# Value projection and states ahead of the query projection in a head's turn

## The chip, the cores and the metric

The kernel runs on one core of a Trainium2 chip. The metric is the device time of the whole kernel in microseconds (us), the median of several runs. Five engines work side by side, each through a queue of its own in program order: TensorE (PE in the profile; PEld are its weight loads), VectorE (DVE), ScalarE (ACT), GpSimd (POOL) and SyncE (SP, which here only issues DMAs). They meet only at semaphores.

## What is computed

One layer of a streaming encoder over 320 tokens: 256 of a prompt (two tiles of 128) and 64 of a running stream. What the change touches is the gated recurrence of its eight heads (128 keys by 128 values each):

```python
proj = jnp.einsum('btd,dn->btn', h, w_in)
q, f_pre, i_v, g_o, u_a, u_b, gate_a, gate_b = jnp.split(proj, SPLITS, axis=-1)
...
# per head: S_t = diag(f_t) S_{t-1} + k_t v_t^T,  o_t = S_t^T q_t
b = jnp.cumsum(logf, axis=2)
attn = jnp.einsum('bhtd,bhsd,bhtsd->bhts', q, k, decay)
o = (jnp.einsum('bhts,bhsv->bhtv', attn, v)
     + jnp.einsum('bhtd,bhdv->bhtv', q * jnp.exp(b), S))
S_new = (jnp.exp(b_last[:, :, 0, :])[..., None] * S
         + jnp.einsum('bhsd,bhsv->bhdv', k_dec, v))
...
o = rms_norm(o, hg_norm_g)
```

Behind it come a convolution branch, the gates, an output projection, a router and sixteen experts.

## The kernel before

**Stages.** Normalisation of the input, then eight **head turns** (from about 20 to 175 us), then the convolution's projections and the gates, the output projections, the router, and the experts from about 355 us to the end. The head turns 0 and 1 are special (`first`, `first_prev`). TensorE runs turns 2 to 7 in a loop of three passes of two turns (L677); ScalarE and VectorE run turns 2 to 5 in a loop and turns 6 and 7 written out.

**A head turn** is a pipeline over three heads: the current head is projected, the levels and the output of the previous one (`prev`) are computed, and the normalisation of the one before that (`pprev`) is finished. On TensorE one turn from the loop is, in this order:

- `cur_f`: 24 matmuls of 128x320, the forget logits, into PSUM bank 0;
- `rms` (L646): a matmul against ones, the sum of squares for `pprev`, into bank 1. It waits for `prev_square` on ScalarE (L1235);
- `levels` (L591): 55 small matmuls of the previous head. It waits for `xr_ready` (VectorE's `query_side`, L1658) and `xk_ready` (GpSimd's `key_side`, L1504);
- `prev_kT` (L614): three transposes;
- `cur_q` (L569): 24 matmuls of 128x320, the query projection, into bank 1. It waits for `rstd_ready`, ScalarE's Ln of bank 1 (L1247), since the sums of `rms` lie in that bank;
- `prev_states` (L622): three matmuls into bank 7;
- `cur_v` (L583): the value projection, into bank 3, 48 passes in the trace;
- `prev_out` (L630): the output of the previous head.

The forget and query projections split inputs and weights into a high and a low part. ScalarE makes the high part of a weight (`w_high`, L1111), VectorE the low one (`w_low`, L1605), and `wlo_ready` counts the low parts.

**ScalarE's turn** is, in this order: `forget` (L1158 to L1164, on the forget logits), `pprev_rms` (L1247, L1248), `key_exp`, `prev_states` (copies of the transposes), `w_high` of the next head's forget weights, `prev_cross`, `q_copy` (L1172: bank 1 to SBUF, signals `q_sb`), `prev_sa` (L1228: first part of bank 7 to SBUF), `level_exp` (L1192: one exponential over 2176 columns, signals `E_ready`), `tile_exp`, `w_high` of the next head's query weights, `v_copy`, `prev_square` (L1235), `store_states` (two DMA issues).

**VectorE's turn**: `forget_in` and the scan, the masks of the previous head, `level_decay` (L1645: seven differences, the input of `level_exp`), `pprev_out`, `w_low` of the next head's forget weights, `prev_final` (L1701, L1703: the new states), `query_side` (L1658: the exponentials times the query, seven instructions), `carry_side`, `w_low` of the next head's query weights. **GpSimd's turn**: `key_decay` (L1490), `level_sums`, `key_side` (L1504, seven instructions).

**SyncE** loads the three weight columns of a head when `v_done` says that the head before the last is projected (L420), and the incoming state when `so_ready` and `o_done` allow it.

The order of the work is written by hand; no scheduler moves anything.

Of the kernel before, what the change touches and what calls it, by code (L numbers as in the profile page):

```python
# [115 lines left out]
def signal(eng, ins, sem, value):  # L116

    ins.then_inc(sem, 1)
    eng.wait_ge(sem, value)


def build(nc, a, o):
    with ExitStack() as ctx:
# [3 lines left out]
        def sem(name):  # L127
            return ctx.enter_context(nc.semaphore(name))
# [44 lines left out]
        def carve(first, *sizes):  # L173
# [65 lines left out]
        cur = [v.rearrange("p (w t e) -> p w t e", w=2, t=3) for v in (cur0, cur1)]  # L239
# [12 lines left out]
        xh_ready, xl_ready, whi_ready, wlo_ready, uhi_ready, ulo_ready, thi_ready, tlo_ready = (  # L252
            sem(n) for n in ("xh_ready", "xl_ready", "whi_ready", "wlo_ready", "uhi_ready", "ulo_ready", "thi_ready", "tlo_ready"))
# [274 lines left out]
        def _(pe):  # L528
            def mm(out, lhsT, rhs, start, stop):
                return pe.matmul(out, lhsT, rhs, start=start, stop=stop)  # L530
# [11 lines left out]
            def project(bank, hi, lo):  # L542

                for k in range(KT):
                    for j, (w, x) in enumerate(((hi, xhk), (lo, xhk), (hi, xlk))):
                        last = mm(ps[:, bank, 0:T], w[:, k * P:k * P + P], x[:, k, :], k == 0 and j == 0, k == KT - 1 and j == 2)
                return last

            def first_f():
                for k in range(KT):  # L550
                    pe.wait_ge(xh_ready, XH[k])
                    if k == 0:
                        pe.wait_ge(xh_ready, XT_A[0])
                    mm(ps[:, 0, 0:T], wh[:, k * P:k * P + P], xhk[:, k, :], k == 0, False)
                for k in range(KT):
                    pe.wait_ge(xl_ready, XL[k])
                    mm(ps[:, 0, 0:T], wh[:, k * P:k * P + P], xlk[:, k, :], False, False)
                pe.wait_ge(wlo_ready, 1)
                for k in range(KT):
                    last = mm(ps[:, 0, 0:T], wl[:, k * P:k * P + P], xhk[:, k, :], False, k == KT - 1)  # L560
                last.then_inc(h["f_done"], 1)

            def cur_f(i, b, first):
                pe.wait_ge(wlo_ready, 2 * (2 * i + b) + 1)
                if not first:
                    pe.wait_ge(h["ls_ready"], 2 * i + b)
                project(0, piece(wh, 0), piece(wl, 0)).then_inc(h["f_done"], 1)

            def cur_q(i, b, first, after_rms):  # L569
                pe.wait_ge(wlo_ready, 2 * (2 * i + b) + 2)  # L570
                if not first:
                    pe.wait_ge(h["q_sb"], 2 * i + b)
                if after_rms:
                    pe.wait_ge(h["rstd_ready"], 2 * i + b - 1)
                project(1, piece(wh, 1), piece(wl, 1)).then_inc(h["q_done"], 1)

            def value_tile(b, t):
                t0, n = TILES[t]
                for k in range(KT):
                    last = mm(ps[0:n, 3, t * P:t * P + P], xT[:, k, t0:t0 + n], sh[:, b, 3, k, :], k == 0, k == KT - 1)  # L580
                return last

            def cur_v(i, b, first):  # L583
                pe.wait_ge(wh_in[b], i * 48 + (16, 48)[b])
                if not first:
                    pe.wait_ge(h["v_sb"], 2 * i + b)
                value_tile(b, 0)
                value_tile(b, 1)
                value_tile(b, 2).then_inc(h["v_done"], 1)
# [24 lines left out]
            def prev_kT(i, b, first):  # L614
                pe.wait_ge(h["kdec_ready"], 2 * i + b + 1)
                if not first:
                    pe.wait_ge(h["so_ready"], 2 * i + b)
                for t, (t0, n) in enumerate(TILES):
                    last = pe.transpose(ps[0:n, 7, t * P:t * P + P], hkde[:, t0:t0 + n], ident)
                last.then_inc(h["kT_done"], 1)  # L620

            def prev_states(i, b):  # L622
                n1 = 2 * i + b
                pe.wait_ge(h["kT_sb"], n1 + 1)
                pe.wait_ge(h["v_sb"], n1 + 1)
                for t, (t0, n) in enumerate(TILES):
                    last = mm(ps[:, 7, t * P:t * P + P], hkT[0:n, t, :], hV[0:n, t, :], True, True)
                last.then_inc(h["s_done"], 1)
# [24 lines left out]
            def head_turn(cur, prev, pprev, first=False, first_prev=False):  # L653

                if first:
                    first_f()
                else:
                    cur_f(*cur, first)
                if first or first_prev:
                    cur_q(*cur, first, False)  # L660
                if first_prev:
                    prev_kT(*prev, True)
                    levels(*prev, True)
                    prev_states(*prev)
                if pprev:
                    rms(*pprev)
                    levels(*prev, False)
                    prev_kT(*prev, False)
                    cur_q(*cur, False, True)
                    prev_states(*prev)  # L670
                cur_v(*cur, first)
                if prev:
                    prev_out(*prev, first_prev)

# [402 lines left out]
        def _(act):  # L1077
# [88 lines left out]
            def q_copy(i, b, first):  # L1166
                n = 2 * i + b
                act.wait_ge(h["q_done"], n + 1)
                if not first:
                    act.wait_ge(h["a_done"], 2 * n - 2)  # L1170
                    act.wait_ge(h["qeb_ready"], n - 1)
                signal(act, act.activation(hq[:, b, :], ps[:, 1, 0:T], ACT.Copy, scale=QSCALE), h["q_sb"], n + 1)  # L1172
# [32 lines left out]
            def prev_states(i, b, first):  # L1205
                n = 2 * i + b
                act.wait_ge(h["kT_done"], n + 1)
                if not first:
                    act.wait_ge(h["s_done"], n)
                pc.turn(n)  # L1210
                pc(act.activation(hkT[:, 0:2, :], ps[:, 7, 0:256].rearrange("p (t n) -> p t n", t=2), ACT.Copy))
                signal(act, act.activation(hkT[0:64, 2, :], ps[0:64, 7, 256:384], ACT.Copy), h["kT_sb"], n + 1)

            def prev_cross(i, b, first):
                n = 2 * i + b
                act.wait_ge(h["am_ready"], 2 * n + 1)
                if not first:
                    act.wait_ge(h["o_done"], n)
                signal(act, act.activation(hAS[0:BLK, 0:2, BLK:P], ps[0:BLK, 4:6, LW:LW + BLK], ACT.Copy), h["ac_ready"], n + 1)

            def prev_sa(i, b, first):

                n = 2 * i + b
                act.wait_ge(h["s_done"], n + 1)
                if not first:
                    act.wait_ge(h["so_ready"], n)
                    act.wait_ge(h["o_done"], n)
                signal(act, act.activation(hSA, ps[:, 7, 0:P], ACT.Copy), h["sa_sb"], n + 1)  # L1228
# [21 lines left out]
            def head_turn(cur, nxt, prev, pprev, first=False, first_prev=False):  # L1250
                forget(*cur, first or first_prev)
                if pprev:
                    pprev_rms(*pprev)
                key_exp(*cur)
                if prev:
                    prev_states(*prev, first_prev)
                if nxt:
                    w_high(*nxt, 0)
                else:
                    u_high(0, 0)  # L1260
                if prev:
                    prev_cross(*prev, first_prev)
                q_copy(*cur, first or first_prev)
                if prev:
                    prev_sa(*prev, first_prev)
                if first:
                    w_high(*nxt, 1)
                level_exp(*cur)
                tile_exp(*cur, first)
                if nxt is None:  # L1270
                    u_high(0, 1)
                    u_high(1, 0)
                    u_high(1, 1)
                elif not first:
                    w_high(*nxt, 1)
                v_copy(*cur, first)
                if prev:
                    prev_square(*prev, first_prev)
                    store_states(*prev)
# [935 lines left out]
```

## Time and profile before

| | us |
|---|---|
| median of 3 runs | 866.62 (865.63 to 866.66) |
| the profiled execution, its own time | 866.5 |
| its span, from the first to the last instruction | 864.6 |
| PE busy | 819.3 (95%) |
| DVE, ACT, POOL busy | 420.4, 239.5, 79.9 |

The span is 2 us shorter than the execution's time. Of the chain that ended last, PE has 60% of the span, DVE 19%, ACT 9% and DMA 9%. In the head turns PE is busy 98% of the time; how the other engines stand in a turn is seen only in their timelines. In a timeline a row shows when the engine started, for how long, and in brackets the idle time ahead of it and what ended that. All matmuls have the line L530, a helper; they are told apart by their tiles: `split_w` are the forget and query projections, `ring,xT` the value projection, `ring` the levels, `cst,ar` at L619 the transposes, `ar,ones` the sum of squares, `ar` x6 the states.

### The profile page before, as it was taken

What the parts mean: (1) busy time and instruction counts of PE and PEld (TensorE: products, weight loads), DVE (VectorE), ACT (ScalarE), POOL (GpSimd) and SP (SyncE); (2) the same over time, 40 slices, a digit from 0 to 9 for tenths busy, and PEclk for the clock granted to TensorE, in tenths of its full rate; (3) what the DMA queues carried; (4) which work ended last, traced back from release to release, by engine and by line L of the source; (5) the groups of instructions that cost most, each with busy time, mean ns of one, the idle gap of its engine ahead of it and who ended that gap; (6) DMA issues with size and microseconds to landing.
All of it is one profiled execution on the core that took longest, in us unless ns stands there. A gap on an engine that the chain in (4) does not pass through costs nothing.

```text
span 864.6 us, 13003 instructions
## 1 busy us (share of the span) xinstructions
PE 819.3 (95%) x5072; PEld 527.6 (61%) x5072; DVE 420.4 (49%) x703; ACT 239.5 (28%) x377; POOL 79.9 (9%) x141
## 2 busy tenths in 40 slices
PE   4999999999999999999999999999999999998892
PEld 2989889989999867576453353534435344352351
DVE  6788889988999973886010201202112021120127
ACT  6666665665455425110101010000100000000011
POOL 1344455430000000000000000000000000000000
PEclk8999999999999999999999999999999999999996
DMA  9322222244333834549979999999999999999991
GB/s 333 144 83 85 82 82 82 106 160 161 135 140 127 338 147 169 225 159 420 423 328 381 430 424 431 428 426 428 427 430 428 428 428 430 427 427 428 428 397 66
DMA packets 33015, 251.09 MB, mean 290 GB/s; under 512 B 4750, under 2 KB 8206, under 8 KB 20938
## 3 DMA queue, kind: packets, MB, share of 16 engines
q1 hardware_dynamic: 30432, 249.17, 70.8%
q10 hardware_dynamic: 2538, 1.32, 0.5%
q8 instruction: 29, 0.48, 0.2%
q14 instruction: 16, 0.13, 0.0%
HBM read 247.99 MB, written 2.48 MB: 290 GB/s over the span
## 4 chain that ended last, share of the span: by engine, by line
PE 60%; DVE 19%; ACT 9%; DMA 9%; issue 2%; ACTq 1%; DVEq 0%; SPq 0%
PE ps L530 58%; DMA ring<-in_w_up_e 8%; DVE ar L1767 4%; DVE ring L1645 4%; DVE split_t L1774 3%; ACT ring L1192 2%; ACT ar L1202 1%; DMA ring<-in_w_in 1%; DVE ar L1681 1%; ACT split_w L1111 1%; DVE ar L1692 1%; PE ps L917 1%; DVE ar L1636 1%; ACTq L1241 1%; ACT ar L1164 1%
## 5 line engine op out<-in xcount | busy, mean ns | idle before, releaser
L530 PE MATMUL ps<-ring,ar 128*64 128x512 f32 (+1 forms) x1056 | 219.4, 569 | 3.3 <-DMA ring<-in_w_gate_e 1.6
L530 PE MATMUL ps<-ring,xT 128*64 128x512 f32 (+2 forms) x896 | 159.9, 459 | 5.3 <-DMA ring<-in_w_gate_e 3.6
L530 PEld LDWEIGHTS ps<-ring,ar 128*64 128x64 f32 x1056 | 73.6, 137 | 133.8 <-issue 123.0
L530 PEld LDWEIGHTS ps<-ring,xT 128*64 128x64 f32 (+1 forms) x896 | 78.6, 152 | 79.0 <-issue 69.2
L530 PE MATMUL ps<-split_x,split_t 128*128 128x320 f32 x672 | 101.1, 311 | 0.5 <-DVE split_t L1774 0.5
L530 PEld LDWEIGHTS ps<-split_x,split_t 128*128 128x128 f32 x672 | 98.6, 188 | 2.5 <-issue 1.4
L2067 DVE TENSOR_TENSOR ar<-ar,ps 128x512 f32<-128x512 f32 (+1 forms) x42 | 28.8, 685 | 137.9 <-PE ps L530 136.1
L530 PE MATMUL ps<-split_x,split_w 128*128 128x320 f32 x480 | 80.0, 323 | 5.9 <-ACT ar L1247 1.8
L530 PEld LDWEIGHTS ps<-split_x,split_w 128*128 128x128 f32 x480 | 73.4, 194 | 10.6 <-ACT split_x L1146 2.1
L1767 DVE SCALAR_TENSOR_TENSOR ar<-ar,params 128x350 f32<-128x350 f32 x116 | 67.7, 584 | 4.1
L2034 DVE SCALAR_TENSOR_TENSOR out_lo<-ps,ar,out_hi 128x1024 fp32r<-128x1024 f32 x7 | 9.0, 1284 | 104.7 <-ACT out_hi L1409 104.7
L530 PE MATMUL ps<-ar 128*64 128x1 f32 (+6 forms) x354 | 48.8, 292 | 0.0
L530 PEld LDWEIGHTS ps<-ar,mid 128*128 128x128 f32 x384 | 43.7, 192 | 7.8 <-issue 7.8
L530 PE MATMUL ps<-ar,mid 128*128 128x128 f32 x384 | 45.4, 277 | 0.0
L530 PEld LDWEIGHTS ps<-ar 128*64 128x64 f32 (+2 forms) x354 | 34.1, 155 | 11.8 <-issue 9.3
L530 PE MATMUL ps<-mid,ring 128*128 128x320 f32 x128 | 34.9, 432 | 0.0
L1490 POOL TENSOR_TENSOR ring<-ar 128x160 f32<-128x160 f32 (+1 forms) x56 | 28.3, 505 | 64.1 <-DVE ar L1636 60.3
L1409 ACT ACTIVATE out_hi<-ps,ar 128x1024 fp32r<-128x1024 f32 x7 | 7.8, 1114 | 94.2 <-PE ps L530 94.2
L2048 DVE TENSOR_TENSOR ar<-ar,ps 128x1024 f32<-128x1024 f32 x7 | 8.6, 1222 | 52.1 <-PE ps L530 52.1
L1392 ACT ACTIVATE ar<-ps 128x1024 f32<-128x1024 f32 x8 | 8.2, 1026 | 91.2 <-PE ps L530 91.2
L1504 POOL TENSOR_TENSOR ring<-ring,ar 128x160 f32<-128x160 f32 (+1 forms) x56 | 30.4, 543 | 25.5 <-ACT ring L1192 16.3
L1658 DVE TENSOR_TENSOR ring<-ring,ar 128x160 f32<-128x160 f32 (+1 forms) x56 | 30.5, 544 | 2.1 <-ACT ring L1192 0.2
(225 smaller groups left out, 839.5 us busy)
## 6 DMA issues: line engine op xcount, KB each, us to landing
ring<-in_w_gate_e SPq DMA_DIRECT2D x31, 2048.0 KB, 20.8
ring<-in_w_up_e SPq DMA_DIRECT2D x31, 2048.0 KB, 16.0
ring<-in_w_down_e SPq DMA_DIRECT2D x26, 2048.0 KB, 19.9
ring<-in_w_in SPq DMA_DIRECT2D x56, 512.0 KB, 4.3
ring<-in_w_down_end SPq DMA_DIRECT2D x3, 2048.0 KB, 35.5
ring<-in_w_o_a SPq DMA_DIRECT2D x8, 512.0 KB, 5.5
ring<-in_w_out SPq DMA_DIRECT2D x1, 4096.0 KB, 14.4
ar<-in_w_down_e SPq DMA_DIRECT2D x6, 512.0 KB, 16.1
```

The costliest lines, as they stand in the source:

```text
L530: return pe.matmul(out, lhsT, rhs, start=start, stop=stop)
L917: last = pe.transpose(ps[:, k // 4, (k % 4) * P:(k % 4) * P + P], eh[:, k * P:k * P + P], ident)
L1111: signal(act, act.activation(piece(wh, q), sh[:, b, q].rearrange("p k n -> p (k n)"), ACT.Copy), whi_ready, 2 * n + q + 1)
L1192: signal(act, act.activation(X[b], X[b], ACT.Exp), h["E_ready"], n + 1)
L1490: ins = pool.tensor_tensor(xv, bv[:, :, hs - 1:hs].to_broadcast([P, w // (2 * hs), hs]), bv[:, :, 0:hs], ALU.subtract)
L1504: ins = pool.tensor_tensor(xv, xv, kv, ALU.mult)
L1645: ins = dve.tensor_tensor(xv[:, :, hs:2 * hs], bv[:, :, hs:2 * hs], bv[:, :, hs - 1:hs].to_broadcast([P, w // (2 * hs), hs]), ALU.subtract)
L1658: ins = dve.tensor_tensor(xv, xv, qv, ALU.mult)
L1767: vc(dve.scalar_tensor_tensor(acc, uc[:, c, j:j + CW], vt[:, c, j:j + 1], acc, ALU.mult, ALU.add))
L1774: signal(dve, dve.tensor_tensor(t_lo[1 - b][q][1], stl[:, b, 8 * q:8 * q + 8].rearrange("p k n -> p (k n)"), t_hi[1 - b][q][0], ALU.subtract),
L2034: signal(dve, dve.scalar_tensor_tensor(out_lo[:, :], ps[:, 6:8, :].rearrange("p b n -> p (b n)"), gs, hiF, ALU.mult, ALU.subtract), e["eos ...
L2067: signal(dve, dve.tensor_tensor(yv, yv, ps[0:c, 4 + j % 2, :], ALU.add), e["y_added"], 6 * n + j + 1 + 6 * late)
```

## The change

On TensorE, in the turns of the loop, the value projection and the states now stand ahead of the query projection. The value projection gets one more wait, for the low part of the current head's query weights: `v_done` frees the buffer from which that part is computed. On ScalarE, in the same turns, the copy of the state `prev_sa` stands ahead of `q_copy`. Turns 0 and 1 keep their order.

```diff
             def cur_v(i, b, first):
                 pe.wait_ge(wh_in[b], i * 48 + (16, 48)[b])
+                pe.wait_ge(wlo_ready, 2 * (2 * i + b) + 2)
                 if not first:
                     pe.wait_ge(h["v_sb"], 2 * i + b)
...
                     rms(*pprev)
                     levels(*prev, False)
                     prev_kT(*prev, False)
+                cur_v(*cur, first)
+                if pprev:
+                    prev_states(*prev)
                     cur_q(*cur, False, True)
-                    prev_states(*prev)
-                cur_v(*cur, first)
                 if prev:
                     prev_out(*prev, first_prev)
...
                 if prev:
                     prev_cross(*prev, first_prev)
+                if prev and not first_prev:
+                    prev_sa(*prev, first_prev)
                 q_copy(*cur, first or first_prev)
-                if prev:
+                if first_prev:
                     prev_sa(*prev, first_prev)
```

TensorE, the second turn of the loop's body from the transposes to the output, before (`split_w` is the query projection, `ring,xT` the value projection, `ar 128x128 x3` ahead of it the states, the last two rows the output):

```order
L619 MATMUL ps<-cst,ar 128x128 x2
L619 MATMUL ps<-cst,ar 64x128
L570 REGISTER_ALU
L530 MATMUL ps<-split_x,split_w 128x320 x24
L530 MATMUL ps<-ar 128x128 x3
L584 REGISTER_ALU
L530 MATMUL ps<-ring,xT 128x128 x16
L530 MATMUL ps<-ring,xT 64x128 x8
L635 ISA
L530 MATMUL ps<-ar 128x128 x3
L530 MATMUL ps<-ar 128x64 x2
```

The same place after:

```order
L620 MATMUL ps<-cst,ar 128x128 x2
L620 MATMUL ps<-cst,ar 64x128
L584 REGISTER_ALU
L585 REGISTER_ALU
L530 MATMUL ps<-ring,xT 128x128 x16
L530 MATMUL ps<-ring,xT 64x128 x8
L530 MATMUL ps<-ar 128x128 x3
L530 MATMUL ps<-split_x,split_w 128x320 x24
L636 ISA
L530 MATMUL ps<-ar 128x128 x3
L530 MATMUL ps<-ar 128x64 x2
```

The query projection moved from right behind the transposes to right ahead of the output.

ScalarE in the same turn, from the cross block's copy (`prev_cross`) to `level_exp`, before (L1172 is `q_copy`, L1228 `prev_sa`, L1192 `level_exp`):

```order
L1219 ACTIVATE ar<-ps 64x2x64
L1170 ISA
L1171 REGISTER_ALU
L1172 ACTIVATE ar<-ps 128x320
L1228 ACTIVATE ar<-ps 128x128
L1192 ACTIVATE ring<-ring 128x2176
L1200 ACTIVATE ar<-ar 128x320
```

The same place after (the lines lie two further down in the file):

```order
L1221 ACTIVATE ar<-ps 64x2x64
L1230 ACTIVATE ar<-ps 128x128
L1172 ISA
L1173 REGISTER_ALU
L1174 ACTIVATE ar<-ps 128x320
L1194 ACTIVATE ring<-ring 128x2176
L1202 ACTIVATE ar<-ar 128x320
```

`q_copy` and `prev_sa` changed places; `q_copy` is now the instruction right ahead of `level_exp`, and it stood ahead of it before too. VectorE, GpSimd and SyncE have the same instructions in the same order as before.

## Rows read from the trace of the kernel before

**Rows 1.** Windows, core 0: stretch, length, busy us of PE, PEld, DVE, ACT, POOL, granted clock, DMA share, GB/s

```profile
75.31:95.26 19.95, 19.57 (x193) 17.81 (x192) 17.20 (x30) 12.56 (x24) 9.46 (x18) 1.00 0.29 90
...
174.50:198.00 23.50, 21.71 (x197) 20.41 (x197) 20.27 (x33) 13.22 (x22) 7.05 (x9) 1.00 0.48 166
```

**Rows 2.** Waits between 56 and 180 us: who waited for whom, total us, times, longest

```profile
ACT ring L1192 <- DVE ring L1645: 24.5, 6, 4.3
...
PE ps L530 <- ACT ar L1247: 1.8, 4, 0.6
```

**Rows 3.** Timeline of TensorE in turn 3: start, length, what, idle before

```profile
79.08 0.78 PE L530 MATMUL ps<-ar,ones 128*128 128x320 f32 x2
79.87 0.92 PE L530 MATMUL ps<-ring 128*64 128x64 f32 x24
...
82.69 0.55 PE L619 MATMUL ps<-cst,ar 128*128 128x128 f32 x3
83.60 3.76 PE L530 MATMUL ps<-split_x,split_w 128*128 128x320 f32 x24 [0.36 <-ACT ar L1247]
87.20 1.02 PE L530 MATMUL ps<-ar 128*128 128x128 f32 x6
88.15 5.73 PE L530 MATMUL ps<-ring,xT 128*128 128x128 f32 x48
93.89 1.44 PE L530 MATMUL ps<-ar 128*128 128x128 f32 x10
...
99.03 0.81 PE L530 MATMUL ps<-ar,ones 128*128 128x320 f32 x2
```

**Rows 4.** Timeline of ScalarE from turn 3 into turn 4

```profile
80.11 0.44 ACT L1158 ACTIVATE ar<-ps 128x320 f32<-128x320 f32 x1 [1.17 <-issue]
...
87.58 0.44 ACT L1172 ACTIVATE ar<-ps 128x320 f32<-128x320 f32 x1 [0.23 <-PE ps L530]
88.30 0.28 ACT L1228 ACTIVATE ar<-ps 128x128 f32<-128x128 f32 x1 [0.28 <-PE ps L530]
92.91 2.02 ACT L1192 ACTIVATE ring<-ring 128x2176 f32<-128x2176 f32 x1 [4.33 <-DVE ring L1645]
...
98.53 0.44 ACT L1235 ACTIVATE ar<-ps 128x320 f32<-128x320 f32 x1
...
100.48 0.44 ACT L1158 ACTIVATE ar<-ps 128x320 f32<-128x320 f32 x1 [1.51 <-issue]
```

**Rows 5.** Timeline of VectorE in turn 3

```profile
88.67 4.16 DVE L1645 TENSOR_TENSOR ring<-ar 128x128 f32<-128x128 f32 x7
...
95.94 3.92 DVE L1658 TENSOR_TENSOR ring<-ring,ar 128x128 f32<-128x128 f32 x7
...
101.39 1.23 DVE L1605 TENSOR_TENSOR split_w<-ring,split_w 128x1024 fp32r<-128x1024 f32 x1
```

**Rows 6.** Timeline of VectorE in turn 1

```profile
55.01 3.92 DVE L1658 TENSOR_TENSOR ring<-ring,ar 128x128 f32<-128x128 f32 x7 [0.17 <-ACT ring L1192]
```

**Rows 7.** Timeline of GpSimd in turn 1

```profile
55.06 4.37 POOL L1504 TENSOR_TENSOR ring<-ring,ar 128x128 f32<-128x128 f32 x7 [3.14 <-issue]
```

**Rows 8.** Timeline of TensorE in turn 2, the first of the loop

```profile
62.58 0.55 PE L619 MATMUL ps<-cst,ar 128*128 128x128 f32 x3
```

**Rows 9.** Timeline of ScalarE, `level_exp` of turn 2 and turn 7, `prev_square` of turn 7

```profile
72.87 2.02 ACT L1192 ACTIVATE ring<-ring 128x2176 f32<-128x2176 f32 x1 [4.21 <-DVE ring L1645]
...
171.70 2.03 ACT L1192 ACTIVATE ring<-ring 128x2176 f32<-128x2176 f32 x1 [3.80 <-DVE ring L1645]
...
179.53 0.44 ACT L1235 ACTIVATE ar<-ps 128x320 f32<-128x320 f32 x1
```

**Rows 10.** Timeline of TensorE behind the last head turn

```profile
180.11 0.78 PE L530 MATMUL ps<-ar,ones 128*128 128x320 f32 x2 [1.79 <-ACT ar L1235]
...
183.64 0.55 PE L619 MATMUL ps<-cst,ar 128*128 128x128 f32 x3
183.94 3.77 PE L530 MATMUL ps<-split_x,split_w 128*128 128x320 f32 x24
```

## The prediction

> **What bounds the kernel now.** First the windows of the head turns: TensorE is busy 19.57 of 19.95 us in turn 3, so it looks like the bound [rows 1]. The waits name what the change aims at: the query projection waits for the Ln of the sums, 1.8 us in four turns [rows 2]. But the same view has a far longer line: ScalarE's `level_exp` waits for VectorE's `level_decay`, 24.5 us in six turns. That idle time is no reserve. `level_exp` stands in a ring of waits of its own: from it ScalarE works straight through to `prev_square`, issues the stores, starts `forget` of the next turn, and VectorE goes on from there to the next `level_decay`. In numbers [rows 4]: `level_exp` 92.91 to the end of `prev_square` 98.97 is 6.06 us, on to `forget` at 100.48 is 1.51 (1.17 ahead of the `forget` at 80.11, where no loop end lies between), and from a `forget` (80.11) to its `level_exp` (92.91) 12.80. Sum 20.0 to 20.4 us, which is what a turn takes: from `level_exp` of turn 2 at 72.87 to that of turn 7 at 171.70 is 98.83, or 19.77 a turn [rows 9]. TensorE's `rms` also hangs on this ring: in turn 4 it starts at 99.03, 0.06 after `prev_square` [rows 3, 4]. So two rings, TensorE's own work and the one over ScalarE and VectorE, are both about a turn long, and what counts is whether the change lengthens a ring through both.
>
> **The edits, one by one.** No matmul is added or removed. The register instructions on TensorE change places; I price them at nothing, as they lie within the gaps between groups counted below.
>
> The *removed wait*: the transposes start at 82.69, the query projection at 83.60 [rows 3]; where nothing held the next group it started 0.30 after the transposes (183.64 to 183.94) [rows 10]. I take 0.35 for a group with other waits. The value projection can then start at 83.04 instead of 83.60, a gain of 0.56 on TensorE's side in such a turn.
>
> The *added wait* in the value projection, for the low query weights, costs nothing: VectorE makes them at the end of its turn, behind `query_side` and `carry_side`, done 6.7 us after `query_side` starts (95.94 to 101.39 + 1.23 [rows 5]), so about 9 us after `level_exp` starts; the value projection stands 10 us after it (sum below). If it did bite, the levels ahead of it would mostly have waited already. Behind it in the queue stand the states, the query and the output. The other waits of the moved groups have been met by then too: the copies of values and transposes are early in ScalarE's turn, and the next turn's loads are issued behind `v_done`, which now comes earlier.
>
> The *moved query projection* is where the cost lies. Its end, and with it `q_copy`, comes later by the value projection (88.15 to 93.89, 5.74) and the states (87.20 to 88.15, 0.95) less the 0.56 won: 6.1 us [rows 3]. `q_copy` started at 87.58 and `level_exp` behind it in the same queue could not start before 92.91 anyway [rows 4], so 5.33 less 0.47 for `q_copy` itself, 4.86, is cover. The rest, 1.2 us, is on the path. Directly for turn 2: transposes 62.58 [rows 8], +0.35 +5.74 +0.95, from a query projection's start to `q_copy` 3.98 (83.60 to 87.58), +0.44 +0.03 gives 74.07 for `level_exp` against 72.87: **1.20 us late**. `level_exp` needs nothing of the query; it is late only because `q_copy` stands ahead of it.
>
> The *swap of prev_sa and q_copy* takes 0.28 us [rows 4] off the way behind `q_copy`, and moves it to where ScalarE waits for the query anyway. Without the swap the price would be that much higher each turn; it is in the sum.
>
> **The new ring.** From then on every turn closes a ring over both engines. From `level_exp` to the end of `prev_square` 6.06 [rows 4]; to `rms` 0.06; `rms` to levels 0.79; levels to transposes 2.82; to the value projection 0.35; value projection 5.74; states 0.95; query projection to `q_copy` 3.98; `q_copy` to `level_exp` 0.47 [rows 3, 4]. Sum **21.22 us**, against 19.77 on average before: 1.45 more in each of the five steps from turn 2 to turn 7, 7.25. With the 1.20 of turn 2: **8.45 us** at the `level_exp` of turn 7.
>
> What is second in line now? `level_decay` would be ready 20.0 to 20.4 after the last `level_exp`, 0.8 to 1.2 us early, so the old ring no longer binds. VectorE's `query_side` began 3.03 us after `level_exp` (95.94 less 92.91) only since VectorE was late with other work [rows 4, 5]; now it can begin as soon as the exponential ends, and GpSimd's `key_side` with it. That happened in turn 1 already: 55.01 for 3.92 and 55.06 for 4.37 [rows 6, 7]. So the keys are done 2.02 + 0.13 + 4.37 = 6.5 us after `level_exp`, 6.7 with a handover of 0.2, and the levels want them at 6.06 + 0.06 + 0.79 = 6.91. A margin of 0.2: it holds, barely.
>
> **What follows the turns.** `rms` of the tail waits for `prev_square` of turn 7 and has waited 1.79 us for it already [rows 9, 10]; that wait gives no cover, since the value waited for is late by the full amount. All that comes after, the convolution, gates and experts with their loads, is released by this work, so I carry the shift to the end whole: 866.5 + 8.45 = 874.95, say **874.9**. The execution of 866.5 is 0.1 under the median of the runs, which changes nothing. A measurement of this kernel can tell about 0.2%, 1.7 us, from no change.
>
> **Bounds of this case.** Low: in the turns that ScalarE has written out the handovers are shorter, and the gap behind the transposes may be 0.30 and not 0.35; 0.25 off in each of five turns and 0.3 off turn 2 gives 6.9, a time of 873.4. High: the gap behind the transposes as long as 0.6 with register work ahead of the value projection, a handover of 0.14 (179.97 to 180.11 [rows 9, 10]) in place of 0.06, and one of 0.1 between `q_copy` and `level_exp`: 0.4 in each of six turns, 2.4 more, or 877.3.
>
> **The rivals.**
>
> *Faster: TensorE's own work is the bound (chance 0.03).* For it: 98% busy [rows 1], and the result of the query projection is not used by VectorE until 95.94 [rows 5]. Then 0.56 us in each of six turns is won, 3.4 us: 863.1. It decides at one point: `q_copy` must be done by 92.9, so the query projection must end by 92.2 in turn 3. On TensorE's sequence it ends at 83.04 + 5.74 + 0.95 + 3.76 = 93.5. I see nothing that brings it 1.3 us earlier. The Trainium skill, page "Perfetto Trace Analysis", section "Optimization Strategy", says to take the most contended engine, find the gaps on it, and make what it waits for start sooner or end sooner. By that rule this change is right and the time falls as in this rival; the trace does not agree that the gap is the limit, since the ring over `level_exp` is as long as TensorE's turn.
>
> *No change (0.04).* The 1.2 us of a turn would be cover that I have missed, or would be given back behind the turns: 866.5 to 868.2. Against it: ScalarE's work between `level_exp` and `prev_square` has no gap, and `rms` starts 0.06 behind it.
>
> *Less, 868.2 to 873.4 (0.08).* The ring closes but is shorter, or part of the shift is absorbed by the loads and the DMA-heavy experts. Each tenth in the ring is worth 0.5 us.
>
> *More, over 877.3 (0.05).* The levels wait for `key_side` or `query_side`, which now run fully side by side. In turn 1 they did so at 3.92 and 4.37 us, as against 3.92 in turn 3 with a later start [rows 5 to 7], so they hardly hold each other up. If they ran one after the other, the levels would start at 2.15 + 3.92 + 4.37 = 10.4 in place of 6.91: 3.5 us in each of five turns, a time of 892. The Trainium skill, page "GPSIMD Engine Reference", section "Key points", states that GpSimd shares its SBUF interfaces with VectorE and contends with instructions of two SBUF inputs, which both of these are. By the rule at its hardest this is the outcome; turn 1 speaks against it.
>
> **How the numbers follow.** The forecast's case, 873.4 to 877.3, has 0.80. I put the range at 872.8 to 877.4, which leaves out both rivals below and most of the two at its edges. Slower by over 0.2% has 0.80 + 0.08 + 0.05 = 0.93, within 0.04, faster 0.03.
>
> **What would show it.** In the profile after: (1) the idle time ahead of `level_exp` is gone, and ahead of `q_copy` ScalarE idles about 3 us for TensorE; (2) TensorE idles 1.4 to 1.6 us ahead of `rms` in turns 3 to 7, released by `prev_square`, and not at all behind the transposes; (3) `level_exp` to `level_exp` 21.2 us; (4) `query_side` starts about 2.1 us after `level_exp`; (5) the granted clock of the turns stays at 1.00, as it did with 1.79 us of idle in the stretch behind them [rows 1]; (6) all behind turn 7 is shifted as a block by about 8 us. I am wrong if `level_exp` still waits for VectorE, if the levels wait for GpSimd or VectorE, or if the shift at turn 7 is not found again at the end.

## The result, and the profile after

The changed kernel takes 877.92 us (median of 4 runs, 875.59 to 879.81) against 866.64 (4 runs): a ratio of 1.0128, 95% interval 1.0116 to 1.0141. It is 11.3 us slower, where 8.45 were forecast, and the median lies 0.5 us above the range. The profiled execution took 878.53 us, 12.0 more than the profiled one of before; its span is 876.7. In the file of after ScalarE's lines lie 2 and VectorE's and GpSimd's 4 further down: `q_copy` is L1174, `prev_sa` L1230, `level_exp` L1194, `prev_square` L1237, `query_side` L1662, `key_side` L1508.

The waits between 56 and 190 us (total us, times, longest), which answer to [rows 2]:

```profile
POOL ring L1508 <- ACT ring L1194: 24.4, 6, 4.6
ACT ar L1174 <- PE ps L530: 21.2, 6, 3.6
ACT ar L1230 <- PE ps L530: 15.7, 6, 3.2
...
PE ps L530 <- ACT ar L1237: 10.8, 7, 4.0
```

The line of 24.5 us, `level_exp` waiting for `level_decay`, is gone. In its place ScalarE waits for the query projection, 3.5 us a turn, and TensorE waits for `prev_square` in every turn. ScalarE's timeline from turn 3 to turn 4 answers to [rows 4]:

```profile
95.37 0.44 ACT L1174 ACTIVATE ar<-ps 128x320 f32<-128x320 f32 x1 [3.57 <-PE ps L530]
95.84 2.02 ACT L1194 ACTIVATE ring<-ring 128x2176 f32<-128x2176 f32 x1
...
101.47 0.44 ACT L1237 ACTIVATE ar<-ps 128x320 f32<-128x320 f32 x1
...
117.02 2.02 ACT L1194 ACTIVATE ring<-ring 128x2176 f32<-128x2176 f32 x1
```

`level_exp` follows `q_copy` by 0.47 us with no wait of its own, and comes back after 21.18 us. TensorE's timeline of the same turn, which answers to [rows 3]:

```profile
84.37 0.55 PE L620 MATMUL ps<-cst,ar 128*128 128x128 f32 x3
84.75 5.63 PE L530 MATMUL ps<-ring,xT 128*128 128x128 f32 x48
90.31 1.13 PE L530 MATMUL ps<-ar 128*128 128x128 f32 x6
91.37 3.78 PE L530 MATMUL ps<-split_x,split_w 128*128 128x320 f32 x24
95.53 1.44 PE L530 MATMUL ps<-ar 128*128 128x128 f32 x10 [0.38 <-DVE mid L1714]
96.90 3.79 PE L530 MATMUL ps<-split_x,split_w 128*128 128x320 f32 x24
101.96 0.81 PE L530 MATMUL ps<-ar,ones 128*128 128x320 f32 x2 [1.28 <-ACT ar L1237]
```

The value projection starts 0.38 after the transposes with nothing in between, so the wait that the change removes is really gone. The idle time has only moved, to the front of `rms`, and has grown. One more wait is new, 0.38 ahead of the output (`pprev_out` on VectorE, L1714), but it ends well inside the time that TensorE then spends waiting for `rms`.

Up to here the chain is as forecast; only the idle time stands in two places. Ahead of `rms` it is 0.76 to 1.74 us in turns 3 to 7, where 1.4 to 1.6 were forecast. Together with the new wait ahead of the output it is 1.65 to 1.77 a turn. What else was not forecast is seen behind the last turn. TensorE, rows that answer to [rows 10]:

```profile
188.71 1.40 PE L530 MATMUL ps<-ar,ones 128*128 128x320 f32 x2 [4.02 <-ACT ar L1237]
190.05 1.55 PE L530 MATMUL ps<-ring 128*64 128x64 f32 x24
...
194.93 0.55 PE L620 MATMUL ps<-cst,ar 128*128 128x128 f32 x3
195.23 3.76 PE L530 MATMUL ps<-split_x,split_w 128*128 128x320 f32 x24
```

The group of 24 level matmuls takes 1.55 us where it took 0.92 a turn earlier and before [rows 3]. From `rms` to the next projection it is 6.52 us (188.71 to 195.23), against 3.83 before (180.11 to 183.94 [rows 10]). The windows (columns as in [rows 1]; the granted clock is the number third from the end) say why:

```profile
75.89:96.90 21.01, 19.47 (x193) 17.83 (x192) 17.34 (x30) 12.44 (x24) 9.69 (x17) 1.00 0.25 86
...
188.70:195.20 6.50, 6.49 (x79) 5.57 (x79) 1.66 (x3) 1.00 (x2) 0.00 (x0) 0.55 0.08 21
```

Granted clock 0.55: TensorE ran at its lower level of 1.2 GHz for most of that stretch, after 4.02 us without work. So the 12.0 us of the profiled execution are: 0.5 us from before the first changed turn (the forget projection of turn 2 starts at 55.29 in place of 54.75), 8.1 us in the turns (`level_exp` of turn 7 at 180.33 against 171.70, less that 0.5), 2.7 us of lower clock, and 0.7 us further behind. The 0.5 are scatter: in experiments 7 and 8, whose code is the same as before up to turn 7, this projection starts at 55.31 and 55.64. The 0.7 lie in the router's part, where the clock fell in both profiled executions, before and after. Its stretch from the small matmuls of 16 columns to the next long group takes 10.57 us before (388.49 to 399.06), 11.27 after (399.74 to 411.01), and 9.31 in the execution of experiment 3, where the clock stayed up there. TensorE after, in that stretch:

```profile
401.58 2.30 PE L530 MATMUL ps<-ar,xT 128*128 128x16 f32 x16
403.72 2.06 PE L530 MATMUL ps<-mid,cst 128*128 128x512 f32 x2
```

The clock falls within the first of these rows (1.00 from 402.0 to 402.8, 0.50 from 403.5 to 409.5), and no idle time is recorded ahead of them. Before, the same first row took 1.85 us, and the clock fell only after the second one and an idle time of 0.76 us (0.56 from 394 to 396).

### The profile page after: what moved, and what is told of

It reads as the page before. It is cut to its first block, busy times and chain, and to the rows that moved or that the text cites. A ratio compares the mean times of both kernels' runs of the same rounds, so it can differ in the third digit from the quotient of the medians.

```text
span 876.7 us, 13004 instructions
## 1 busy us (share of the span) xinstructions
PE 824.6 (94%) x5072; PEld 532.2 (61%) x5072; DVE 421.7 (48%) x703; ACT 239.4 (27%) x377; POOL 80.6 (9%) x141
## 4 chain that ended last, share of the span: by engine, by line
PE 69%; DVE 14%; DMA 8%; ACT 7%; issue 1%; ACTq 0%; SPq 0%; DVEq 0%
PE ps L530 67%; DMA ring<-in_w_up_e 8%; DVE ar L1771 5%; DVE split_t L1778 3%; ACT ring L1194 2%; ACT ar L1204 1%; ACT split_w L1113 1%; DVE ring L1649 1%; PE ps L919 1%; DMA ar<-in_x_prompt 1%; DVE ring L1558 1%; DVE mid L1788 0%; DVE ring L1563 0%; PE ps L620 0%; PE ps L909 0%
## 5 line engine op out<-in xcount | busy, mean ns | idle before, releaser
L1508 POOL TENSOR_TENSOR ring<-ring,ar 128x160 f32<-128x160 f32 (+1 forms) x56 | 30.9, 551 | 33.5 <-ACT ring L1194 24.4
L1662 DVE TENSOR_TENSOR ring<-ring,ar 128x160 f32<-128x160 f32 (+1 forms) x56 | 30.5, 544 | 5.7 <-ACT ring L1194 4.0
```

The lines of the kernel that those rows point to most:

```text
L1508: ins = pool.tensor_tensor(xv, xv, kv, ALU.mult)
L1662: ins = dve.tensor_tensor(xv, xv, qv, ALU.mult)
```

## The experiments

Every run was timed beside the kernel before on the same chip; the kernel before had medians of 866.45, 866.3 and 867.03 us in the three groups.

**1. The changed kernel once more.**

> The changed kernel once more, as the standard for the others of this call: 877 to 878.5 us. Theory: about 8.4 us come from the turns (level_exp to level_exp 21.1 us) and about 2.7 us from TensorE at its lower clock (granted 0.55 between 191 and 195 us) behind the 4.0 us idle ahead of the first rms after the turns. If that is so, a run in which the clock does not fall there should show 875 us.

876.89 us (875.12 to 878.38). The two executions with a mean clock of 0.991 took 875.49 and 875.12 us, the two with 0.980 and 0.981 took 878.30 and 878.38. That points to the clock, but the mean is a weak sign: the kernel before has means of 0.984 to 0.993 in the three groups, and its times do not follow them. The step between `level_exp` of turn 2 (74.78) and turn 6 (159.38) is 21.15 us a turn. But from turn 6 to turn 7 it is 22.60 (159.38 to 181.98), and the windows show that the clock fell in a second place, in turn 7, behind an idle time of only 1.72 us ahead of `rms`:

```profile
165.50:171.00 5.50, 5.43 (x79) 4.95 (x80) 4.30 (x8) 4.12 (x8) 0.36 (x1) 0.69 0.51 187
190.30:195.70 5.40, 5.34 (x78) 4.56 (x79) 1.44 (x2) 1.00 (x2) 0.00 (x0) 0.68 0.09 26
```

My expectation knew of one place only. The step of turn 7 grew by 1.5 us, and behind the last turn `rms` to the next projection took 5.37 us.

**2. Filling TensorE's idle time behind the last turn.**

```diff
             conv_value(0)
+            pe.wait_ge(h["q_sb"], 8)
+            project(1, u_hi[0][0][1], u_lo[0][0][1])
             rms(3, 0)
```

> The changed kernel, with one more projection (24 matmuls of 128x320, 3.8 us) on TensorE in the 4.0 us in which it idles behind the last turn; its result in bank 1 is overwritten by rms and never read, so the outputs are the same. Theory (the clock fell because of that idle time): the granted clock stays at 1.00, rms and levels take 3.8 us in place of 6.5, and the time is 2.7 us below the changed kernel, 875.0 to 875.4. Rival (the 2.7 us are lost whatever TensorE does, or the added matmuls themselves delay rms): 877.5 to 879.

876.10 us (874.00 to 877.43), 0.8 below the changed kernel of the same group, so the number I gave was missed. The profiled execution explains it: where the idle time was filled the clock stays up, and `rms` to the next projection is back at 3.84 us; in turn 7, where nothing was filled, it fell again. Windows of turn 7 and of the tail:

```profile
165.20:170.70 5.50, 5.46 (x79) 4.99 (x80) 4.30 (x8) 4.12 (x8) 0.33 (x1) 0.69 0.52 194
190.00:194.00 4.00, 3.95 (x80) 3.47 (x81) 1.60 (x2) 1.00 (x2) 0.00 (x0) 1.00 0.12 35
```

In this execution the mechanism holds for its own place, and the theory had to take in the second.

**3. Filling both places.**

```diff
                 if pprev:
+                    pe.wait_ge(h["q_sb"], 2 * cur[0] + cur[1])
+                    mm(ps[:, 1, 0:T], ones, xT[:, 0, :], True, True)
                     rms(*pprev)
                     levels(*prev, False)
```

and the tail's filling as above.

> The changed kernel with TensorE's idle time filled in both places where its clock was seen to fall: the extra projection behind the last turn as in the run with the filled tail, and in turns 2 to 7 one extra matmul of 128x320 against ones (0.78 us) ahead of rms, whose result rms overwrites. The added work is never read, so the outputs are the same. Theory (all that the changed kernel costs above the ring's 8.4 us is the clock in these two places): granted clock 1.00 from 30 to 350 us, every execution near 874.5 (873.8 to 875.2), none of the 877 to 879 that the changed kernel and the filled tail also show. Rival (the spread comes from elsewhere, the experts' loads or the start): the same 874 to 877.4 as with the filled tail alone.

874.12 us, and the five executions lie within 873.76 and 874.79. Granted clock over all of the turns and the stage behind them:

```profile
30.00:350.00 320.00, 311.91 (x2447) 283.59 (x2446) 267.48 (x433) 174.51 (x271) 77.82 (x136) 1.00 0.36 128
```

TensorE does more work here than in the changed kernel, and the kernel is faster and no longer spreads: 874.12 against 876.89, which is 2.8 us across two groups, or 2.5 us by the two ratios to the kernel before. The result of the added matmuls is never read, so they can pay only by way of the clock. Not all of the gain need be theirs: the router's stretch, where nothing was filled, takes 9.31 us in this execution and 10.69 in that of experiment 1. What is left over the kernel before is a ratio of 1.0084 (1.0070 to 1.0098), some 7 us beside the 8.45 computed; `level_exp` of turn 7 stands at 179.88 against 171.70, with the same 21.14 us a turn.

**4. `level_exp` ahead of `q_copy`.**

```diff
                 if prev and not first_prev:
                     prev_sa(*prev, first_prev)
+                    level_exp(*cur)
                 q_copy(*cur, first or first_prev)
...
-                level_exp(*cur)
+                if first or first_prev:
+                    level_exp(*cur)
```

> The changed kernel with level_exp ahead of q_copy on ScalarE in turns 2 to 7, TensorE's order as changed. Theory (the loss in the turns comes only from level_exp standing behind q_copy, which waits for the query projection): the ring through TensorE opens, what remains is ScalarE's ring with q_copy's 0.47 us now inside it, 20.2 us a turn, and 869 to 869.8 us with the clock at 1.00. Rival (the order on TensorE costs by itself, levels or query_side start late since the query ends later): 21 us a turn and 874 or more.

870.33 us (868.56 to 872.80), 6.6 below the changed kernel, with the same order on TensorE. ScalarE in turn 3:

```profile
93.64 2.02 ACT L1194 ACTIVATE ring<-ring 128x2176 f32<-128x2176 f32 x1 [2.74 <-DVE ring L1651]
95.82 0.44 ACT L1174 ACTIVATE ar<-ps 128x320 f32<-128x320 f32 x1 [0.17 <-ACT ring L1194]
```

`level_exp` waits for VectorE again, as in [rows 4], and comes every 20.32 us (73.10 to 174.69 in five steps; 20.2 expected). The median is 0.5 above what I gave, and for a reason met already: behind the last turn TensorE idles 2.62 us, the clock falls, and `rms` to the next projection takes 6.72 us in the profiled execution; the one with a mean clock of 0.993 took 868.56. So the loss in the turns does not come from TensorE's order as such. It comes from the place of one copy in ScalarE's queue: the turn is 0.8 us shorter than in the changed kernel, and the 0.55 us that it is still above 19.77 are about the 0.47 of that copy, which now stands behind `level_exp` in ScalarE's own ring.

**5 and 6. Each half of the change alone.** First TensorE's part, with ScalarE's old order (`q_copy`, then `prev_sa`):

> TensorE's new order with ScalarE's old one (q_copy, prev_sa, level_exp). Theory: prev_sa's 0.31 us (0.28 and a handover) come into the ring in six turns: 1.9 us above the changed kernel, 879.5 to 880.5. Rival (the copies behind the query don't lie on the path): as the changed kernel, 877.5 to 878.5.

878.52 us (877.49 to 879.02), 1.6 above the changed kernel of the same group where 1.9 was forecast; the absolute figure was too high, since the changed kernel itself ran 1 us lower there. A turn is 21.44 us (74.82 to 182.01 in five steps), 0.3 more than 21.14. Then ScalarE's part alone, in TensorE's old order:

> TensorE's old order with prev_sa ahead of q_copy on ScalarE. Theory: q_copy starts about 1 us later (behind the states, 88.6 in place of 87.6 in turn 3) but level_exp starts at 92.9 as before, since it waits for level_decay: 866.6, no change. Rival (every delay of q_copy counts): 6 us more.

866.26 us, a ratio of 0.9996 (0.9987 to 1.0005). ScalarE in turn 3:

```profile
88.44 0.28 ACT L1228 ACTIVATE ar<-ps 128x128 f32<-128x128 f32 x1 [0.93 <-PE ps L530]
88.88 0.44 ACT L1172 ACTIVATE ar<-ps 128x320 f32<-128x320 f32 x1 [0.17 <-ACT ar L1228]
93.06 2.02 ACT L1192 ACTIVATE ring<-ring 128x2176 f32<-128x2176 f32 x1 [3.74 <-DVE ring L1647]
```

`q_copy` comes 1.3 us later than in [rows 4] and it costs nothing: 3.74 us of cover are left. So a delay of `q_copy` within the prediction's cover is free, as far as this run used it.

**7 and 8. The kernel before, with more idle time behind the last turn.** Two copies on ScalarE, or one:

```diff
                     u_high(1, 0)
+                    act.wait_ge(wu_in[1], 32)
+                    act.wait_ge(h["a_done"], 14)
+                    for _ in range(2):
+                        step(act.activation(u_hi[1][1][1], su[:, 1, 1].rearrange("p k n -> p (k n)"), ACT.Copy))
                     u_high(1, 1)
```

> The kernel before, with two more copies of 128x1024 on ScalarE (1.09 us each, the same values written again) behind the last turn's level_exp, so that prev_square of turn 7 comes 2.2 us later and TensorE idles 4.0 us in place of 1.8. Theory (that idle time makes the clock fall): granted clock about half in rms and levels behind it, and 2.2 + 2.7 = 4.9 us more than before, 871.5. Rival (idle time of that length leaves the clock alone): 2.2 us more, 868.8.

870.86 us (868.88 to 871.32): 4.6 above the kernel before, for 2.2 us of added work.

> As the last one with one added copy of 1.09 us: TensorE idles 2.9 us. Theory: if 2.9 us of idle time leaves the clock alone, 1.1 us more than before, 867.7; if it falls, 1.1 + 2.7, 870.4. I expect the first in most executions.

869.48 us (868.34 to 872.05): 3.2 above the kernel before, for 1.1 us. I had expected the clock to stay up here in most executions; in the profiled one it did not. TensorE with one copy:

```profile
182.00 1.40 PE L530 MATMUL ps<-ar,ones 128*128 128x320 f32 x2 [2.92 <-ACT ar L1235]
183.34 1.55 PE L530 MATMUL ps<-ring 128*64 128x64 f32 x24
...
188.60 3.77 PE L530 MATMUL ps<-split_x,split_w 128*128 128x320 f32 x24
```

6.60 us from `rms` to the next projection, at a granted clock of 0.54. That execution is the slowest of its six (872.05); even the fastest, 868.34, is 2.0 us above the kernel before for 1.1 us of work, but what its clock did is not known. These two runs have nothing of the change in them, and their medians lie 2.4 and 2.1 us above what the added work alone would give. In the two profiled executions the clock behind the turns has 1.5 us (two copies) and 2.8 us (one) of that. So the clock is a price of idle time on TensorE in this place, whatever makes it.

**9. The next query weights' high part ahead of `level_exp`, in the kernel before.**

```diff
-                if first:
-                    w_high(*nxt, 1)
-                level_exp(*cur)
-                tile_exp(*cur, first)
                 if nxt is None:
                     u_high(0, 1)
                     u_high(1, 0)
                     u_high(1, 1)
-                elif not first:
+                else:
                     w_high(*nxt, 1)
+                level_exp(*cur)
+                tile_exp(*cur, first)
```

> The kernel before, with ScalarE's high parts of the next query weights (1.06 us a turn; three such copies in turn 7) moved from behind level_exp and tile_exp into the 4.3 us in which ScalarE waits for level_decay. Theory (in the kernel before the ring over ScalarE and VectorE is the bound, and TensorE's own 19.3 us come next): turns of 19.3 us in place of 19.8, and no wait behind turn 7: 2.3 + 1.8 = 4.1 us less, 862.5. Rival (TensorE is the bound already): only the 1.8 us behind turn 7, 864.8, or nothing.

862.42 us (861.76 to 863.69), a ratio of 0.9956 (0.9943 to 0.9970) to the kernel before. It was run again in the last group:

> The kernel before with the high parts moved early once more, on this chip: 862.4 us, 0.4 to 0.5% under the kernel before.

862.12 us, a ratio of 0.9947 (0.9934 to 0.9961). This is the fastest version of the study, with TensorE's old order. The size is as forecast, the split is not, so the agreement is in part luck. `level_exp` of turn 2 is 0.84 earlier (72.03 for 72.87) as turn 1 already gains; the steps are 19.58 us (72.03 to 169.91 in five) and not 19.3; and the wait of 1.79 us behind the last turn is gone. Of the 0.95 us that the five steps give, 0.57 come in the last, written-out one; inside the loop 1.06 us less work for ScalarE shortens a turn by about a tenth (turn 3 to turn 4, 20.21 for 20.34). The waits between 56 and 190 us say what holds the turn there:

```profile
ACT ring L1192 <- DVE ring L1643: 16.9, 6, 3.6
ACT ar L1158 <- PE ps L530: 8.3, 6, 1.8
```

ScalarE's `forget` now waits for the forget projection, and TensorE in turns 3 to 5 waits 0.38 to 0.69 us ahead of the output and 0.21 to 0.51 ahead of the levels, both times for VectorE. So the ring through ScalarE was the bound from turn 1 to turn 2 and behind the last turn. In the loop's turns another ring over VectorE and TensorE is nearly as long; no run takes that one apart.

**10. The same move in the changed kernel.**

> The changed kernel with the same move on ScalarE that made the kernel before 4 us faster: the high parts of the next query weights ahead of level_exp. Theory: they need the query projection's end, which in the new order comes right ahead of level_exp, so the 1.06 us stay in the ring, only ahead of the exponential and not behind it: turns of 21.1 us and 876 to 878, no gain. Rival (the move helps in either order): 4 us less than the changed kernel, 873.

886.26 us (884.61 to 888.08): neither. It is 8 to 9 us slower than the changed kernel in the other groups (877.92, 876.89), and both theories were wrong. The turn is 23.67 us (`level_exp` at 100.05 and 123.72). TensorE in between:

```profile
105.06 0.81 PE L530 MATMUL ps<-ar,ones 128*128 128x320 f32 x2 [1.89 <-ACT ar L1237]
106.88 1.55 PE L530 MATMUL ps<-ring 128*64 128x64 f32 x24 [1.01 <-POOL ring L1506]
```

`level_exp` starts 1.1 us later against TensorE's work, and the levels now wait for GpSimd's `key_side`, which starts when it ends. I had moved 1.06 us from behind the exponential to ahead of it and looked at `prev_square` only; the second way from `level_exp` to TensorE, over `key_side` to the levels, had next to no margin. On top, the clock fell in turns 3 to 6 (0.74 from 105.0 to 111.5), behind idle times of 1.89 to 2.00 us ahead of `rms` and 0.70 to 1.01 ahead of the levels. In numbers, from turn 3 to turn 4: the levels start 6.83 us after `level_exp`, as in the changed kernel (6.86), so moving the copy ahead of it takes nothing off behind it and adds its 1.06 us. The levels up to the transposes take 4.25 us in place of 2.82, by the lower clock. Together 2.5 us, which is what the turn is longer (23.67 against 21.14).

## Why the prediction was right and wrong

**What bounds the kernel: right.** Two rings of about a turn each. Experiment 9 shortened ScalarE's and the time fell, but inside the loop by only a tenth of a us a turn, which fits a second ring of nearly the same length. That second ring is not TensorE's own work alone, as the prediction has it: VectorE stands in it.

**The removed wait: right and worth nothing.** The value projection starts 0.38 us behind the transposes (0.35 taken).

**The added wait: right,** no idle time stands ahead of the value projection; the low part is done at 104.77 and the projection starts at 105.91.

**The moved query projection: right, and in size.** Turn 2 was to be 1.20 us late; `level_exp` stands at 74.63 against 72.87, of which 0.54 had come in before, 1.22 in all. The ring was to be 21.22 us and is 21.14 (74.63 to 180.33 in five steps). The turns were to cost 8.45 and cost 8.1 in the profile. Experiment 4 shows the named cause, the place of `q_copy`; experiment 6 shows the cover.

**The swap on ScalarE: right,** 0.3 us a turn (experiment 5).

**The step that failed** stands under "What follows the turns": "I carry the shift to the end whole", with the expectation that the granted clock stays at 1.00. I counted TensorE's wait for `prev_square` of turn 7 as 1.79 us, as before; it became 4.02 us. In the new order the forget projection ahead of that `rms` starts 0.57 us behind `level_exp` of turn 7 (180.90 against 180.33), where it started 2.83 us behind it (174.53 against 171.70). So TensorE is through 2.26 us earlier against ScalarE's chain, and these add to the 1.79: 4.05. I could have had that from my own terms: output and forget projection follow the query projection by fixed times. And I took the clock at 1.00 from one stretch with 1.79 us of idle time, which says nothing of 4. A term for the clock was put at nothing. What it costs: 2.7 us in the profiled execution (6.52 less 3.83), 1.5 us in another (5.37 less 3.83), and 1.5 us more where it falls in turn 7 too. The router's part adds 0.7 in the profiled execution, which the change did not demonstrably cause. Without the clock the forecast of 874.9 meets the executions with the highest mean clock, 875.1 to 875.6, which were not profiled, and the filled kernel with 874.1, which was.

**The rivals.** That TensorE is the bound, and that nothing changes, are ruled out by the result. The rival of more, in which the levels wait for GpSimd or VectorE, did not occur in the changed kernel: TensorE's matmuls wait for neither in any turn (one weight load waits 0.4 us for `query_side`), and `query_side` and `key_side` start together there and take what they took in [rows 6, 7]:

```profile
97.95 3.90 DVE L1662 TENSOR_TENSOR ring<-ring,ar 128x128 f32<-128x128 f32 x7 [0.41 <-ACT ring L1194]
```

with 4.35 us for GpSimd's seven from 97.99. But my reason against this rival, that the two groups hardly hold each other up, was wrong. In turn 3 of the kernel before they overlapped too, all but VectorE's last instruction. Taken one by one, VectorE's last two of the seven there (the same form, GpSimd's group ends at 99.31) are:

```profile
98.84 0.65 DVE L1658 TENSOR_TENSOR ring<-ring,ar 128x160 f32<-128x160 f32 x1
99.53 0.33 DVE L1658 TENSOR_TENSOR ring<-ring,ar 128x160 f32<-128x160 f32 x1
```

0.65 us beside GpSimd and 0.33 alone. So the contention that the Trainium skill states for two SBUF inputs (page "GPSIMD Engine Reference", section "Key points") is seen in these groups: VectorE's instructions take about twice as long. It was already in the 3.92 and 4.37 us that the sum uses, before and after, and so cost nothing new; the rival's 3.5 us counted it a second time. The margin that I gave for this wait as 0.2 us was smaller: `key_side` ends at 102.34 and the levels start at 102.70, and in experiment 10, where they do wait for it, the same handover is 0.35 (106.53 to 106.88). That the wait did not bite was close to luck.

## What to carry to other kernels

A wait on the busiest engine is not the bound because it is visible there: lay out every ring of waits, and for a group that moves ask which copy waits for it and what stands behind that copy in an in-order queue. Idle time of another engine, here ScalarE's 4.3 us ahead of `level_exp`, is where work can be put for nothing, provided that its inputs are there by then (experiments 9 and 10). What it gains stops at the next ring of the same length. And a sum that makes TensorE idle longer needs a term for its clock: compute the new idle time at each place, and look for the nearest row with as much.

## What the runs showed of the hardware

I had not expected that so little idle time can go ahead of a fall of TensorE's clock. These are the idle times ahead of `rms` and what the profiled execution shows in the 5 to 7 us behind them:

| kernel | place | idle, us | granted clock | `rms` to the next projection, us |
|---|---|---|---|---|
| before | behind the turns | 1.79 | 1.00 | 3.83 |
| filled in both places | turn 7 | 1.21 | 1.00 | 3.91 |
| after, first execution | turn 7 | 1.74 | 1.00 | 3.91 |
| after, once more | turn 7 | 1.72 | 0.69 | 5.46 |
| filled tail | turn 7 | 1.75 | 0.69 | 5.46 |
| `level_exp` first | behind the turns | 2.62 | 0.52 | 6.72 |
| before, one copy more | behind the turns | 2.92 | 0.54 | 6.60 |
| TensorE's part alone | behind the turns | 3.05 | 0.70 | 5.36 |
| before, two copies more | behind the turns | 3.93 | 0.68 | 5.35 |
| after, first execution | behind the turns | 4.02 | 0.55 | 6.52 |
| after, once more | behind the turns | 4.02 | 0.68 | 5.37 |

The next projection is the value projection in turn 7. The same idle time in the same place gave both outcomes (1.72 and 1.74). The cost of a fall in this table is 1.5 to 2.9 us and does not grow with the idle time: 4.02 us gave both 2.7 and 1.5. The same kernel has executions from 875 to 880 us, and with both places filled they agree within 1 us. That the falls make this spread is likely but not shown, since of the changed kernel only two executions, of 878.5 and 878.4 us, were profiled; falls in the router's part can have a share in it.

The Trainium skill, page "TensorE: Matmul & The Clock Gate", section "What's actually happening", says that a gate lets a part of the clock's pulses through by how busy the engine has been. In the head turns the traces agree in that: idle time came ahead of each fall, and filling it removed them. In the router's part of the changed kernel no idle time is recorded ahead of the fall, only matmuls of 16 columns; there the traces leave open what the gate counts as busy. When exactly the clock falls is left open too.
